# A linear-attention mixer: the differential attention's steps begin at tabled slots, four per head from slot 2 on, and the first triangular levels are issued ahead of them

## The reference, cut to what matters

```python
def diff_attention(...):                       # 6 heads, two softmax maps per head, 4 query blocks of 128
    s = q_blk . k - slope * distance           # scores for both maps, 128 x 512 each
    p = softmax(s)
    a = p[:, 0] - lam * p[:, 1]
    return a . v

def chunk_gated_delta(q, k, v, g, beta):       # 6 heads, both directions, chunks of 64 tokens
    A = strictly_lower(kb . k * decay)
    sol = triangular_solve(I + A, [v*beta, kb*exp(gc)])     # per chunk
    def step(state, chunk):                    # 8 chunks, one after the other
        v_new = u - w . state
        o = qg . state + Aqk . v_new
        state = state * gl + kdec . v_new
```

## Time and profile before

| what | value |
|---|---|
| median of 3 runs | 3787.8 us (3787.16 to 3788.26) |
| profiled execution, its own time | 3787.34 us |
| its span, first to last instruction | 3785.6 us |
| mean granted TensorE clock | 0.986 of full speed |
| mixer of layer 0, on TensorE | 2271.0 to 2508.5 us |
| mixer of layer 1, on TensorE | 3103.0 to 3338.4 us |
| share busy: PE, PEld, DVE, ACT, POOL | 96%, 80%, 57%, 41%, 9% |

### The profile page before, as it was taken

The page is one execution under the profiler, slowest core; times in us unless marked ns, Lnnn a source line. Parts: engine busy times, 40 slices in busy tenths (PEclk is TensorE's granted clock), DMA queues, the critical chain, the costliest instruction groups (busy, mean ns, idle before and its releaser), DMA issues. The chain is left out here.

```text
span 3785.6 us, 58644 instructions
## 1 busy us (share of the span) xinstructions
PE 3650.9 (96%) x24913; PEld 3014.9 (80%) x24913; DVE 2164.9 (57%) x3353; ACT 1537.3 (41%) x2423; POOL 337.5 (9%) x325
## 2 busy tenths in 40 slices
PE   7999899999999999999999998999999999999998
PEld 4887688888888888878888776777888777778887
DVE  4734766455466444474227766745377866644375
ACT  3224632111354322253226435643266436633364
POOL 0030220000000000000000005510000014400000
PEclk9999899999999999999999998999999999999999
DMA  5530013333212111122223311013232311022231
GB/s 194 179 105 5 7 46 112 123 123 123 86 62 78 64 56 54 65 89 89 92 86 100 102 45 43 19 47 99 87 103 89 91 51 26 19 83 84 89 101 67
DMA packets 262767, 301.24 MB, mean 80 GB/s; under 512 B 9371, under 2 KB 229426, under 8 KB 262514
## 3 DMA queue, kind: packets, MB, share of 16 engines
q1 hardware_dynamic: 260433, 293.41, 24.2%
q10 hardware_dynamic: 2080, 4.19, 0.3%
HBM read 284.14 MB, written 2.10 MB: 76 GB/s over the span
## 5 line engine op out<-in xcount | busy, mean ns | idle before, releaser
L536 PE MATMUL banks<-h_halves,w_halves 128*128 128x512 f32 x3708 | 1370.4, 370 | 14.2 <-DVEq L428 10.6
L538 PE MATMUL banks<-h_halves,w_halves 128*128 128x512 f32 x3708 | 1364.7, 368 | 0.0
L540 PE MATMUL banks<-h_halves,w_halves 128*128 128x512 f32 x3708 | 1359.5, 367 | 0.0
L536 PEld LDWEIGHTS banks<-h_halves,w_halves 128*128 128x128 f32 x3708 | 699.0, 189 | 146.3 <-issue 13.9
L540 PEld LDWEIGHTS banks<-h_halves,w_halves 128*128 128x128 f32 x3708 | 697.3, 188 | 119.2
L538 PEld LDWEIGHTS banks<-h_halves,w_halves 128*128 128x128 f32 x3708 | 698.6, 188 | 115.6 <-issue 1.4
L263 DVE TENSOR_TENSOR w_halves<-work,w_halves 128x2048 fp32r<-128x2048 f32 (+1 forms) x212 | 482.8, 2277 | 484.9 <-ACT w_halves L258 484.9
L258 ACT ACTIVATE w_halves<-work 128x2048 fp32r<-128x2048 f32 (+1 forms) x212 | 401.8, 1895 | 387.1 <-PE banks L540 363.4
L258 ACT ACTIVATE h_halves<-kept 128x512 fp32r<-128x512 f32 (+1 forms) x520 | 332.9, 666 | 281.4 <-PE banks L540 235.6
L263 DVE TENSOR_TENSOR h_halves<-kept,h_halves 128x512 fp32r<-128x512 f32 (+1 forms) x514 | 356.9, 736 | 137.0 <-ACT h_halves L258 135.8
L1130 DVE SCALAR_TENSOR_TENSOR kept<-kept 128x512 f32<-128x512 f32 x280 | 189.8, 751 | 10.3 <-DMA kept<-in_mod_w 10.3
(11 more groups left out here) (415 smaller groups left out, 4693.0 us busy)
## 6 DMA issues: line engine op xcount, KB each, us to landing
work<-in_w_ff SPq DMA_DIRECT2D x64, 1024.0 KB, 5.3
work<-in_ffn_w_in SPq DMA_DIRECT2D x44, 1024.0 KB, 5.0
kept<-in_mod_w SPq DMA_DIRECT2D x40, 1024.0 KB, 5.2
work<-in_odd_w_in SPq DMA_DIRECT2D x24, 1024.0 KB, 5.2
work<-in_w_in SPq DMA_DIRECT2D x24, 1024.0 KB, 5.2
work<-in_ffn_w_out SPq DMA_DIRECT2D x16, 1024.0 KB, 5.2
work<-in_even_w_in SPq DMA_DIRECT2D x13, 1024.0 KB, 5.4
work<-in_odd_w_out SPq DMA_DIRECT2D x8, 1024.0 KB, 5.1
```

What stands on the lines that cost most here:

```text
L536: nc.tensor.matmul(o, low[:, k - a, fc], rh[:, tc], start=opens, stop=False, skip_group_check=shared)
L538: nc.tensor.matmul(o, high[:, k - a, fc], rl[:, tc], start=False, stop=False, skip_group_check=shared)
L540: mm = nc.tensor.matmul(o, high[:, k - a, fc], rh[:, tc], start=False, stop=(k == K - 1), skip_group_check=shared)
```

## The change

Steps begin where a table says. `begins = [LV * h + 2 * i + 2 ...]` gives each head its four steps at slots 7h+2, 7h+4, 7h+6 and 7h+8; the last one and the next head's first one are one slot apart. Nothing of the attention stands ahead of the loop any more, the 14 dummy matmuls of the opening go, and 4 dummy matmuls stand in each of slots 1 to 4, between `pairs` and `products`. `weigh` goes ahead of the first `turn_step` of the same slot, and `out` ahead of `copy`. VectorE does lambdas and memsets ahead of `update(0, 0)`, and `query_gram(0)` and `queries(0, ...)` inside slots 1 to 3. `results_of_states` moves from lv 5 to lv 6.

```diff
+    begins = [LV * h + 2 * i + 2 for h, i in steps]
+
     def step_at(t, lag):
 
-        s, odd = divmod(t + 2 - lag, 2)
-        return s if odd == 0 and 0 <= s < N else None
+        return begins.index(t - lag) if t - lag in begins else None
...
-                    if lv == 5:
+                    if lv == (6 if h < H else 5):
                         results_of_states(h - 1)
...
-                    for s, work in ((step_at(t, 3), lambda s: turn_step(s, 0)), (step_at(t, 4), weigh)):
+                    for s, work in ((step_at(t, 4), weigh), (step_at(t, 3), lambda s: turn_step(s, 0))):
...
-            pe.wait_ge(loads_in, 96)
-            scores(0)
-            core.hold(7, 14)
...
+                    if 0 < t < 5:
+                        core.hold(7, 4)
                     if h < H and lv:
                         products(h, lv)
...
-            exps(0)
             for t in range(slots):
...
+                if step_at(t, 4) is not None:
+                    out(step_at(t, 4))
                 if step_at(t, 3) is not None:
                     copy(step_at(t, 3), 0)
-                if step_at(t, 4) is not None:
-                    out(step_at(t, 4))
...
             key_gram(0)
-            update(0, 0)
             dve.wait_ge(loads_in, 96)
             lambdas()
...
-            top(0)
-            lambdas_difference()
-            query_gram(0)
-            for d in range(2):
-                queries(0, d)
+            update(0, 0)
             for t in range(slots):
...
                 if h < H and t:
                     update(h, lv)
+                if t == 1:
+                    query_gram(0)
+                    lambdas_difference()
+                if t in (2, 3):
+                    queries(0, t - 2)
```

## The result

| | before | after |
|---|---|---|
| median | 3788.69 us (3782.95 to 3795.46, 15 runs) | 3796.76 us (3789.79 to 3810.19, 15 runs) |
| ratio to before, 95% interval | | 1.0023 (1.0012 to 1.0033) |
| profiled execution, its own time | 3787.34 us | 3810.19 us |
| its mean granted clock | 0.986 | 0.977 |

The change made the kernel slower, by 8.1 us between the medians, where 10.6 us less was forecast. The 15 runs of after lie far apart, and their times go with their clocks: 3789.8 us at a mean granted clock of 0.983, 3810.2 at 0.977. The profiled execution is the slowest of them, so its rows show the loss larger than the medians do; the runs show the same thing by their clocks.

A forecast was written before the change was run, and what follows sets the result against it. TensorE, busy 96% of the span, was taken as the bound. Layer 0 gains 9.9 - 3.5 = 6.4 us, layer 1 7.7 - 3.5 = 4.2, together 10.6: 3787.8 - 10.6 = 3777, range 3767 to 3788 (the forecast's own 3771 to 3782).

The forecast's parts named there:

- Heads 1 to 5: Heads after the first and last slots: waits 5.0 us above the earlier 11.0, 1.5 counted back, net loss 3.5 per layer.
- rival 2: First head: clock falls as in the old one, taking back 6 to 14 us, 3783 to 3791; chance 0.18.
- The one fall that I counted back: Start of the last seven slots: one fall to half clock goes with its waits, 1.5 us back.
- sign of being wrong: First head's granted clock staying near 0.7, or `turn` and `results` waits in levels 3 and 4 passing 3 a head.
- The rule that was weighed: First head: short matmul bursts with waits between throttle the array again; 7.0 us of waits in 31.6 would bring falls.
- The first head: Slots 0 to 6: 24.6 us of work plus 7.0 of new waits, 9.9 less in layer 0, 7.7 in layer 1.
- slot 7 beginning: Sign to look for: slot 7 begins some 31.6 us after the token turns.
- (f): First head, slot 6: a wait for `update` of 0.4 us, among 7.0 of new waits.
- The price of half clock: First head: a us at 1.2 GHz costs at least 0.31 us, from comparing the two layers.
- Rival 1: First head: no clock falls, dummies hide some 8 of the 14 us of new waits, 3769; chance 0.16.
- Rival 3: Level 3 of heads 1 to 4: VectorE becomes the bound, 2.5 us a head, 20 in all, 3797; chance 0.10.
- Rival 4: Whole loop: gain only put off, delayed attention caught up and last steps set the end, 3788; chance 0.06.

The follow-up runs named there:

- e3: The changed kernel with `split(2)` one step earlier, in level 0 of head 3 where it ran before: 3783.32 us, ratio 0.9988.
- e1: The changed kernel with dummy matmuls in heads 1 to 4, four at the end of level 3, two ahead of `results` in level 4: 3773.97 us.
- e2: The changed kernel without its dummy matmuls in slots 1 to 4: 3801.18 us, ratio 1.0039.
- e5: The changed kernel with another table: late start kept, steps caught up by slot 17, old rhythm from step 10 on: 3772.59 us, ratio 0.9961.
- e6: The changed kernel with four dummy matmuls behind level 4's work in heads 1 to 4, waits left open: 3810.86 us, ratio 1.0047.
- e8: The changed kernel with `results_of_states` in level 5 again: 3808.14 us, ratio 1.0048.
- e7: The changed kernel with the table of e5, the dummies of e1, and `query_gram(0)`, lambda difference and `queries(0, ...)` ahead of the loop: 3770.74 us.

## Why the prediction was wrong

**The step that failed** is the sum of "Heads 1 to 5": "Against the 11.0 of before that is 5.0 more" and "Net loss 3.5 in each layer". Behind the first head after needs 201.7 us in layer 0 where before had 181.4. Less the 4.8 of moved attention that is a loss of 15.5, and 21.4 in layer 1 (207.8 against 181.5), where 3.5 stood. I had put some 12 us of short waits into these heads, mostly in levels 3 to 5, and priced them at their length alone. New half clock behind them stood at nothing; rival 2 looked for the clock in the first head only. In the runs that term is the loss: behind the first head after has 44.4 and 58.0 us at half clock where before had 6.8 in each layer, and at 0.44 the difference is 16.5 and 22.5, all of the loss to within about a us. The experiments point the same way: with `split(2)` back, head 3 waits 0.9 us less and takes 10.6 less (e3); with 4.3 us of waits filled, a mixer takes 11.4 less (e1). The one fall that I counted back, at the start of the last seven slots, did go: head 5 and those slots stand at 1.00, 52.2 us where before had 54.9. Neither sign of being wrong that the prediction named came: the first head stood at 1.00, and `turn` and `results` waited 1.4 a head at most. One sign watched the clock of the first head and the other the length of waits, and the loss lay in neither.

**The rule that was weighed** (the Trainium skill, TensorE: Matmul & The Clock Gate, "HAM oscillation — how this bites in real kernels") was set against the first head. The section's case is short bursts with waits for DMA that outlast them. In the kernel before the trace agrees: the clock fell at 2287.3, inside the wait of 4.84 for the stacks. The new first head has no such wait; it stayed at 1.00 with 6.6 us of waits in 26.0, none over 1.8, and it needed its dummies for that: in e2 it fell to 0.70. I then took the later heads as safe because the waits of before had left them at 1.00; I did not ask what 1.0 more at one place in each would do. A second section of that page, "A second HAM failure mode: psum-queue depth-cycling", tells of a bf16 kernel whose frequent short idle times between groups of matmuls made the clock go down and up. The falls in heads 3 and 4, behind waits of 2.22 and of 0.96 and 0.37 between groups, agree with it.

**The first head** came out as walked, 26.0 and 26.3. The prediction's 31.6 kept 4.8 us of moved attention in for the balance, so its own figure for "slot 7 beginning" should have read 26.8. Less its waits the head is 19.4, for the 19.8 of the single groups. The new waits were 0.8, 1.8, 1.7, 1.2 and 1.1, 6.6 in all for 7.0. Off were `weigh` (1.2 for 1.9), `update` of slot 6 (1.1 for 0.4) and slot 4, where 0.4 was counted and no wait has a row.

**The later waits** sum to 12.8 by the rows. The 11.0 of the earlier trace rows has in it the wait of 0.4 at the start of slot 7, which also stands as (f) in the first head; without it before had 10.6, so 2.2 were new where 5.0 was counted: `turn` 1.0 in three heads instead of four, `results` 0.4 instead of 0.7, head 3 behind `split(2)` 3.4 for 2.3.

**The price of half clock**, at least 0.31, is 0.44. At 0.44, and with the 6.8 us at half clock in the opening that I had left out, the old first head would have been 41.52 - 23.9 × 0.44 = 31.0 at full clock, or up to 1.4 more for the 3.2 us that lie in its wait. In rival 2 the middle of 0.31 and 0.5 is 0.405 and not 0.42, which leaves its 14 as it is.

**The rivals.** Rival 1, no falls, is what e5 and e1 come near to: 3772.6 and 3774.0 for its 3769, though the first head's waits did not hide in the dummies. Rival 2 had the mechanism and the wrong place. Rival 3 had the right side and the size, 3797, by luck, since its reason was wrong: VectorE's chain in level 3 costs TensorE 1.0 a head where 2.3 was needed, and e1 keeps VectorE's order and wins. Rival 4 is out, since e5 keeps the late start and its gain.

**Open:** why a fall lasts 20 us and more in after, mostly 10.2 in e3 and e6 and 3.4 in the later heads of before, and which of two identical heads falls (e2, head 2). In layer 0 of after head 4 falls and heads 1 and 2, with the same waits, do not. In e6 dummies behind the wait go with shorter falls, but e8 has the same falls in layer 0 (3.4, 10.2, 10.2, 17.1 and 10.2) without them, so the dummies are not shown to be the cause.

## What to carry to other kernels

Price a new wait on TensorE twice: its length, and the half clock that may follow it; here waits of 1 to 2 us came ahead of stretches of 20 us at half clock in some heads and not in others, and each us of these cost 0.44. After a change of order, read the granted clock head by head before any wait list, and where a short wait cannot be removed, put dummy matmuls into it, not behind it. If runs of one kernel spread by half a per cent, set their times beside their clocks before looking for the cause in the order of the work.

## What the runs showed of the hardware

- The granted clock stayed at 0.50 for 23.9 and 20.5 us while TensorE was busy for 93% and 97% of the time, in groups of small tiles. It rose in level 6 of both heads.
- Fifteen runs of the same kernel spread from 3789.8 to 3810.2 us along clocks of 0.983 to 0.977.
- The same head, with the same matmuls and nearly the same waits, stood at 1.00 in one layer and fell in the other: 32.33 and 41.01 us for head 2 in one run (e2).
- In e7 two `queries` (64 x 512) took 2.44 us on VectorE, where one alone took 0.68 in after, and an operation of 128 x 1 took 1.08. GpSimd worked almost without pause through the two `queries` of e7 and stood idle during that one of after; whether that is what slowed them was not tested.
